# Moving the border inside a tile's mixing in a layer that gathers expert rows

## The reference

```
h = layer_norm(x)
proj = h @ w_in                                # 2824 columns
y_a = window_attention(q, k, v, sinks)         # 8 heads, window of two chunks of 64
y_b = gated_rmsnorm(gated_delta_rule(silu(conv(qkv))), z)   # 4 heads of 128, state over chunks
h = layer_norm(ALPHA * h + concat(y_a, y_b) @ w_out)
scores = (h @ w_query) . sub_keys              # 8 heads x 2 x 128 keys
expert = top 16 of the sums of the top 16 of both halves    # 128 experts for each token
act = gelu(expert_u[expert] . h) * softmax(best)
out = layer_norm(ALPHA * h + sum(act * expert_v[expert]))
```

## Time and profile before

| | |
|---|---|
| time, median of 3 runs | 3772.17 us (3769.79 to 3791.0) |
| the profiled execution: time | 3825.0 us |
| its span, first to last instruction | 3823.2 us |
| mean granted TensorE clock | 0.731 of full speed |
| busy: PE, DVE, POOL, ACT | 2165.8, 2152.2, 2080.4, 380.1 us |
| moved by DMA | 1191.73 MB, mean 312 GB/s |

### The profile page before, as it was taken

One profiled execution on the slowest core, in us unless ns is written; L12 is line 12 of the kernel. 1 busy time (PEld: TensorE's weight loads), 2 busy tenths in 40 slices (PEclk: granted clock), 3 DMA queues, 4 the chain that ended last, 5 costly groups with the idle time before them and its releaser, 6 DMA issues. The chain is left out here.

```text
span 3823.2 us, 34475 instructions
## 1 busy us (share of the span) xinstructions
PE 2165.8 (57%) x9905; PEld 1092.6 (29%) x9905; DVE 2152.2 (56%) x6670; ACT 380.1 (10%) x697; POOL 2080.4 (54%) x2079
## 2 busy tenths in 40 slices
PE   6999967646656566735663554556653333323355
PEld 4665745224243232213321231123211000100111
DVE  4342567766667676566755765577656554444300
ACT  3321132011010010001000100010000000000000
POOL 0000046646536566666665656666656666666664
PEclk9999988767767767767776677667776565555677
DMA  8423168978859799989998999889989999999997
GB/s 281 133 77 109 48 216 298 361 263 334 321 182 362 282 330 388 379 335 338 356 399 325 342 333 403 337 322 355 404 326 362 352 365 360 348 364 369 349 369 291
DMA packets 400102, 1191.73 MB, mean 312 GB/s; under 512 B 54737, under 2 KB 122658, under 8 KB 397986
## 3 DMA queue, kind: packets, MB, share of 16 engines
q0 software_dynamic: 294912, 1073.87, 75.0%
q1 hardware_dynamic: 39970, 75.66, 5.5%
q10 hardware_dynamic: 65024, 39.89, 3.6%
HBM read 1168.27 MB, written 21.00 MB: 311 GB/s over the span
## 5 line engine op out<-in xcount | busy, mean ns | idle before, releaser
L948 POOL DMA_INDIRECT U<-in_expert_u,eidx x1024 | 1046.8, 1022 | 556.5 <-issue 286.0
L1330 PE MATMUL bank<-V,ZH 128*32 128x512 f32 x3712 | 714.0, 887 | 918.2 <-DMA V<-in_expert_v,eidxT 717.5
L2094 DVE CUSTOM_DVE_ANT_0 U<-U,h1c 128x512 f32<-128x512 f32 x1368 | 871.3, 689 | 538.6 <-DMA U<-in_expert_u,eidx 432.2
L956 POOL DMA_INDIRECT V<-in_expert_v,eidxT x832 | 835.3, 1004 | 549.3 <-POOLq L954 302.2
L1330 PEld LDWEIGHTS bank<-V,ZH 128*32 128x32 f32 x3712 | 141.4, 141 | 1394.1 <-issue 1392.0
L2083 DVE CUSTOM_DVE_ANT_0 U<-U,h1c 128x1024 f32<-128x1024 f32 x256 | 303.2, 1224 | 58.9 <-DMA U<-in_expert_u,eidx 42.5
L304 PE MATMUL bank<-V,U 128*128 128x387 f32 (+2 forms) x1056 | 316.1, 459 | 12.4 <-PEq L302 12.2
L978 POOL COPY eidx<-eidx_n 128x128 uint32<-128x128 uint32 x8 | 3.4, 430 | 443.2 <-POOLq L977 443.2
L304 PEld LDWEIGHTS bank<-V,U 128*128 128x128 f32 x1056 | 201.3, 193 | 117.4 <-issue 20.8
L1135 PE MATMUL bank<-wq,arena 128*128 128x512 f32 x400 | 197.1, 642 | 47.7 <-PEq L1258 32.7
L1088 PE MATMUL bank<-arena 128*128 128x512 f32 x224 | 124.8, 704 | 39.0 <-DMA arena<-in_w_out 17.3
(11 more groups left out here) (301 smaller groups left out, 2726.5 us busy)
## 6 DMA issues: line engine op xcount, KB each, us to landing
arena<-in_w_out SPq DMA_DIRECT2D x56, 512.0 KB
U<-in_w_in ACTq DMA_DIRECT2D x36, 512.0 KB, 3.9
U<-in_expert_u,eidx POOLq DMA_INDIRECT x1024
V<-in_expert_v,eidxT POOLq DMA_INDIRECT x928
raw<-proj_dram SPq DMA_DIRECT2D x8, 1344.0 KB
wq<-in_w_query SPq DMA_DIRECT2D x4, 2048.0 KB, 16.1
proj_dram<-U ACTq DMA_DIRECT2D x42, 192.0 KB, 1.9
arena<-w_dram SPq DMA_DIRECT2D x6, 1024.0 KB
```

What stands on the lines that cost most here:

```text
L948: pool.indirect_dma_start(U[:, c % NU, :], None, expert_u[0], rows(ap=eidx[:, e, c:c + 1], axis=0)).then_inc(g_u[c % NU], 16)
L956: pool.indirect_dma_start(V[:, c % NV, :], None, expert_v[0], rows(ap=eidxT[:, e, token:token + 1], axis=0)).then_inc(g_v[c % NV // 2], 16)
L1330: last = nc.tensor.matmul(acc_ps[NSTEP * j:NSTEP * j + NSTEP, 512 * n:512 * n + 512], Zb[:, at - i:at - i + NSTEP], buf[j][:, 512 * n:512 ...
L2094: ins = nc.vector.tensor_tensor_reduce(out=U[:, c % NU, lo:lo + D // 2], in0=U[:, c % NU, lo:lo + D // 2], in1=rows[:, lo:lo + D // 2], sc ...
```

## The change

The point at which a segment takes over a tile's mixing moves from its start to its middle. A loop segment t now does pieces 12 to 36 of tile t + 1 (table `BACK`, halves 9 to 38; PE starts with piece 11 at half 8), then the tail of tile t + 1 (`TAIL`, halves 40 to 57), and beside it pieces 0 to 11 of tile t + 2 (`FRONT`, halves 39 to 61; piece 11 of PE comes in the next segment). Segment 1 does only pieces 0 to 11 of tile 3 (`NEXT_FRONT`, halves 31 to 62), and tile 2's tail is placed somewhat otherwise (`FIRST_TAIL`, 32 to 56). Segment 6 (`ahead` = 1) does pieces 12 to 36 and the tail of tile 7. At the head of a segment PE waits for the new values of the chunk (`b_vnew`) where it had waited for the scores to be read; that wait now stands at PE's half 40. ACT copies the next tile's rows (`rows_ahead`) behind its piece 22 and no more at the head of the segment. SP's list in a turn becomes: first two slices (`first_slices`), the store, the residual rows and the other slices of tile t + 3, and then raw of tile t + 4. DVE no longer waits for the store in piece 1 (`b_pr_free` is gone).

```diff
--- before.py
+++ after.py
@@ -80,18 +80,16 @@
 LATE_MIX = phase(list(range(7, 23)) + list(range(31, 37)),
                  [1, 2, 4, 5, 7, 8, 10, 11, 12, 13, 15, 15, 16, 17, 18, 20, 25, 26, 27, 28, 29, 30])
 LATE_MIX_PE = tensor_phase(LATE_MIX, **route_phase(21, 2), n35=31)
-NEXT_MIX = phase(list(range(23)) + list(range(31, 37)),
-                 [31, 33, 34, 35, 36, 37, 38, 39, 40, 41, 43, 44, 45, 46, 47, 48, 49, 51, 51, 53, 55, 56, 57,
-                  61, 61, 63, 63, 63, 63])
-NEXT_MIX_PE = tensor_phase(NEXT_MIX, **route_phase(59, 2))
-FIRST_TAIL = phase(range(37, 50), [33, 34, 38, 40, 42, 44, 46, 48, 50, 52, 54, 60, 61])
-FIRST_TAIL_PE = {48: 60, 49: 62}
-MIX = phase(list(range(23)) + list(range(31, 37)),
-            [7, 9, 11, 13, 15, 17, 19, 21, 23, 25, 27, 29, 31, 33, 35, 36, 37, 39, 39, 41, 43, 45, 47,
-             53, 55, 57, 59, 61, 63])
-MIX_PE = tensor_phase(MIX, **route_phase(49, 1))
-TAIL = phase(range(37, 50), [1, 3, 10, 14, 18, 20, 22, 26, 28, 30, 32, 50, 52])
-TAIL_PE = {48: 51, 49: 54}
+FIRST_TAIL = phase(range(37, 50), [32, 33, 35, 36, 38, 40, 41, 43, 44, 46, 47, 55, 56])
+FIRST_TAIL_PE = {48: 53, 49: 57}
+NEXT_FRONT = phase(range(12), [31, 34, 37, 39, 42, 45, 48, 51, 54, 57, 60, 62])
+NEXT_FRONT_PE = tensor_phase({n: half for n, half in NEXT_FRONT.items() if n < 11})
+BACK = phase(list(range(12, 23)) + list(range(31, 37)), [9, 11, 13, 14, 15, 17, 17, 19, 21, 23, 25, 31, 32, 35, 36, 37, 38])
+BACK_PE = tensor_phase(BACK, n11=8, n35=40, **route_phase(27, 1))
+TAIL = phase(range(37, 50), [40, 42, 44, 45, 45, 46, 46, 48, 48, 50, 50, 56, 57])
+TAIL_PE = {48: 55, 49: 60}
+FRONT = phase(range(12), [39, 41, 43, 45, 47, 49, 51, 53, 55, 57, 59, 61])
+FRONT_PE = tensor_phase({n: half for n, half in FRONT.items() if n < 11})
 FOLD_SLOT, FOLDS = 1, 2
 SUM_AT, ROWS_AT = 4, 6
 CONVS = range(6, 18)
@@ -749,7 +747,6 @@
         b_wo_free0 = sem("b_wo_free0")
         b_wo_free1 = sem("b_wo_free1")
         b_pre_in = sem("b_pre_in")
-        b_pr_free = sem("b_pr_free")
         b_pr_done = sem("b_pr_done")
         b_tok_raw = sem("b_tok_raw")
         b_squared = sem("b_squared")
@@ -896,11 +893,17 @@
                     sp.dma_start(raw[:, :, :], proj_dram[:, :, bass.ts(t, P)]).then_inc(b_raw, 16)
                     sp.dma_start(akt[:, :], ak_dram[:, bass.ds(t * P, CHUNK + P)]).then_inc(b_raw, 16)
 
-                def more_loads(t):
+                def first_slices():
+                    for k in range(2):
+                        sp.wait_ge(b_wo_free1 if k % 2 else b_wo_free0, 1)
+                        sp.sem_inc(b_wo_free1 if k % 2 else b_wo_free0, -1)
+                        sp.dma_start(wo[k % 2], wo_v[k]).then_inc((b_wo1 if k % 2 else b_wo0), 16)
+
+                def more_loads(t, first=0):
                     sp.wait_ge(b_pr_done, 1)
                     sp.sem_inc(b_pr_done, -1)
                     sp.dma_start(pre[:, :], h_dram[t]).then_inc(b_pre_in, 16)
-                    for k in range(KD - 2):
+                    for k in range(first, KD - 2):
                         if k == 4 and streamed(t):
                             sp.wait_ge(w_stored, 16)
                             sp.wait_ge(w_free, 1)
@@ -928,13 +931,18 @@
                         sp.wait_ge(b_projected, 1)
                         sp.sem_inc(b_projected, -1)
                     loads(t)
-                    more_loads(t)
+                    if t < 3:
+                        more_loads(t)
                 with sp.Fori(0, T - 4) as t:
+                    first_slices()
+                    store(t)
+                    more_loads(t + 3, 2)
                     loads(t + 4)
-                    store(t)
-                    sp.sem_inc(b_pr_free, 1)
-                    more_loads(t + 4)
-                for t in range(T - 4, T - 1):
+                first_slices()
+                store(T - 4)
+                sp.sem_inc(t_free, 1)
+                more_loads(T - 1, 2)
+                for t in range(T - 3, T - 1):
                     store(t)
                     sp.sem_inc(t_free, 1)
                 store(T - 1)
@@ -1365,12 +1373,13 @@
                         for half in (2 * s, 2 * s + 1):
                             if ahead > 0:
                                 at(TAIL_PE, half, t + 1)
+                                at(BACK_PE, half, t + 1)
                             if ahead > 1:
-                                at(MIX_PE, half, t + 2)
+                                at(FRONT_PE, half, t + 2)
                         weighted(t - 1, s)
                         if s == 0:
                             if ahead > 0:
-                                piece(35, t + 1)
+                                pe.wait_ge(b_vnew, 1)
                             norm_rows(2, t_ln)
 
                 pe.wait_ge(b_load, 80)
@@ -1408,7 +1417,7 @@
                     for half in (2 * s, 2 * s + 1):
                         at(LATE_MIX_PE, half, 2)
                         at(FIRST_TAIL_PE, half, 2)
-                        at(NEXT_MIX_PE, half, 3)
+                        at(NEXT_FRONT_PE, half, 3)
                     if s % 2:
                         weighted(0, NSTEP // 2 + s // 2)
                 with pe.Fori(0, T - 4) as t:
@@ -1601,16 +1610,17 @@
                     weights()
                     root()
                     norm()
-                    if ahead > 0:
-                        act.wait_ge(b_hx_free, 1)
-                        act.sem_inc(b_hx_free, -1)
-                        rows_ahead()
                     for s in range(USEG):
                         for half in (2 * s, 2 * s + 1):
                             if ahead > 0:
                                 at(TAIL, half, t + 1)
+                                at(BACK_PE, half, t + 1)
+                                if BACK_PE[22] == half:
+                                    act.wait_ge(b_hx_free, 1)
+                                    act.sem_inc(b_hx_free, -1)
+                                    rows_ahead()
                             if ahead > 1:
-                                at(MIX_PE, half, t + 2)
+                                at(FRONT_PE, half, t + 2)
                         if 4 <= s <= 24 and s % 4 == 0:
                             fill(1 + s // 4)
 
@@ -1829,8 +1839,6 @@
                         dve.wait_ge(s_dve, 1)
                         dve.sem_inc(s_dve, -1)
                         dve.sem_inc(b_root_in, 1)
-                        dve.wait_ge(b_pr_free, 1)
-                        dve.sem_inc(b_pr_free, -1)
                         pad()
                         soften(0, t)
                     elif n == 2:
@@ -2170,12 +2178,12 @@
                         elif half == ROWS_AT + 1:
                             norm()
                         if ahead > 0:
+                            at(BACK, half, t + 1)
                             at(TAIL, half, t + 1)
                         if ahead > 1:
-                            at(MIX, half, t + 2)
+                            at(FRONT, half, t + 2)
 
                 dve.sem_inc(b_raw_free, 1)
-                dve.sem_inc(b_pr_free, 4)
                 dve.sem_inc(b_h1n_free, 1)
                 dve.sem_inc(w_yfree, 1)
                 dve.sem_inc(g_accfree, 1)
@@ -2211,7 +2219,7 @@
                     dot(1, 2 * half + 1)
                     at(LATE_MIX, half, 2)
                     at(FIRST_TAIL, half, 2)
-                    at(NEXT_MIX, half, 3)
+                    at(NEXT_FRONT, half, 3)
                 with dve.Fori(0, T - 4) as t:
                     segment(t + 2, 2)
                 segment(T - 2, 1)
```

## The result

The changed kernel takes 3823.46 us (median of 4 runs, 3806.63 to 3837.43) where the kernel before takes 3781.59 us (3769.79 to 3792.03): ratio 1.0106, 95% interval 1.0063 to 1.015. It is slower, by 1.1%, and the interval excludes a ratio of 1; the forecast was 3705 us and faster, with a range that ended at 3778. The profiled execution of the changed kernel took 3806.6 us, 17 us under its median, and that of before 3825.0, 43 us over its own. So the two traces, laid side by side, show a gain of 18 us that the timed runs don't have, and a segment of the first comparison may carry several us of luck: segment 7, which is the same in both kernels, differs by 6. Later traces were needed for the sizes.

A forecast was written before the change was run, and what follows sets the result against it. The prediction took segment 1 to be bound by DVE's chain and the loop to sit 20 to 30 us above its gathers; -64 + 15 - 20 = -69 on the profiled 3825.0 gave 3756, about 3705 as median, range 3650 to 3778.

The forecast's parts named there:

- What bounds the kernel now: Whole kernel: segment 1 bound by DVE's chain, loop segments some 20 to 30 us above the pace of their gathers.
- Part 1: Segment 1: pieces 12 to 22 and 31 to 36 of tile 3 leave it, -64 us (bounds 50 to 75).
- Part 2: Segment 6: it gets pieces 12 to 36 of tile 7 and 5.6 MB of loads, +15 us (bounds +5 to +30).
- Part 3: Loop segments 2 to 5: new order of pieces gives 395 us each, -5 a segment, -20 for four.
- The 198: Loop segment, halves 31 to 58 (top-k, tail, pieces 0 to 9): 198 us, between 158 of work alone and 219.
- halves 0 to 8 need 29 (the rows fetched ahead cover them): Loop segment, first nine halves: 29 us once pieces 37, 38 and 0, about 14 us, are removed.
- rival (c): Segment 1 gains, but loop segments take 405 to 412 us and give back half to all: 3742 to 3772; chance 0.24.
- Rival (b): Crowded stretch paces everything at 8.2 us a half: loop segment 426 us, +55 in all, 3827; chance 0.10.
- its turning point: Rival of the pacing stretch: the sign turns when a loop segment exceeds 413 us, from 7.7 us a half.
- Rival (a): Crowded stretch hidden under the gathers: loop segments 380 us, -129 in all, 3643; chance 0.08.
- Rival (d): Segment 1 keeps its length, bound by PE or the front pieces' chain: gain 25 instead of 64, 3742; chance 0.06.
- The conversion: Whole kernel: profiled execution 53 us above the runs' median, same difference taken after, so 3756 becomes about 3705.

The follow-up runs named there:

- fast chip: Pace of two groups of follow-up runs, in which the kernel before takes 3513 or 3514 us and a gather 1.29 us.
- b_again: The kernel before, unchanged, timed and traced again in the first follow-up group: 3513.02 us, ratio 1.0006.
- b_more: The kernel before with ten more DVE reductions (13 us in all) in halves 20 to 29 of segments 2 to 7: 3529.75 us, ratio 1.005 to before.
- slow chip: Pace of the other groups of runs, in which the kernel before takes 3782 to 3812 us and a gather 1.42 to 1.46 us.
- two later pairs: Kernel before and changed kernel, both unchanged, traced again: 3513.02 and 3558.15 us in one group, 3823.08 and 3841.55 us (one execution each) in another.
- a_again: The changed kernel, unchanged, timed and traced again in the first follow-up group: 3558.15 us, ratio 1.013 to before.
- the pair at 1.44: Kernel before and changed kernel, both unchanged, traced in the fourth follow-up group, one execution each: 3823.08 and 3841.55 us.

## Why the prediction was wrong

**What bounds the kernel now: read wrongly in part.** "Halves 0 to 38 with DVE as the pacer" rested on a share of 0.84 to 0.93 and the absence of waits for rows. In the trace of the same kernel on the fast chip the waits are nearly as rare in halves 9 to 30 (5.0 us) and the share is 1.02. The forecast sought part of its gain in the 20 to 30 us above the bare gathers; b_again shows 21.5 of them at full DMA, and b_more that two thirds of added work is hidden. For the slow chip of the forecast's own trace this is not tested.

**Part 1: right.** Forecast -64, measured -58 (407.0 to 348.6), and -68 and -70 in the two later pairs. The second half was forecast at 168 us and took 167.4.

**Part 2: right in sign, small.** +15 forecast, +26, +13.5 and +22.9 measured, within +5 to +30. I charged it to bytes; on the fast chip that charge fits (13.9 us for 13.5), on the slow ones it leaves some 8 to 11 us without a cause.

**Part 3: the step that failed.** The sum for a loop segment was 29 + 131 + 198 + 22 + 14 = 394. Measured in segment 3: 48.4 for halves 0 to 8, 130.7 for 9 to 30, 198.0 for 31 to 58, 31.1 for the rest with the border, 408.2 in all. The terms for halves 9 to 30 and for the crowded stretch hold to the microsecond, the last two together are 5 less. The 198 had luck in it: it was picked between 158 and 219, and the other loop segments have 197 to 204. The failed step is "halves 0 to 8 need 29 (the rows fetched ahead cover them)". The 29 are before's 43 us less the 14 of the pieces that left: DVE's work. But nine halves of gathers take 9 x 5.8 = 52 us, and the eight rows of U cover four halves of them, 23 us, only if the ring is full at the border. In before it was filled there, while DVE stood at the border and worked through the top-k (halves 59 to 63 took 54.8 us, five halves of gathers 29), and POOL stopped 9.4 us because no U row was free, so it was full. DVE then ran at 4.8 us a half on rows already there. In the changed kernel the ring fills in the crowded stretch and is drawn down right behind it: halves 51 to 58 took 33.9 us on the fast chip, where gathers need 41. At the border no more rows stand ahead: DVE waited for them, 10.1 us for landings in this trace (15.1 in a_again) and 8 us with no releaser that the profile shows, 5.4 us a half. I took away the stop and kept its yield. So the segment is gathers' pace plus DVE's excess in the crowded stretch, less what the ring gives back behind it (7 of 27 us on the fast chip).

By that account the loss should grow as gathers get faster: it was +25 us a segment at 1.29 us a gather, +16 in the pair at 1.44 and +6 in the first, where single executions differ by several us. The first pair of traces, with loop segments of 406.2 us and 18 us gained in all, is rival (c), at a chance of 0.24: its reason, a bunch of pieces against a ring of four halves, is the one shown here. The timed runs and the later pairs go beyond it. Rival (b) had the mechanism and the sign, at a chance of 0.10 and a pace of 8.2 us a half; 7.1 was enough, because its turning point was worked out with the same wrong 29 us. Rival (a) gave 380. The stretch's busy time is 147 of 198 us in the first trace and 147 of 172.7 on the fast chip, where 28 halves of gathers are 145: the busy time alone would just fit. Over it come, on the fast chip, 8.3 us for landings in halves 31 to 38 and 18 us of handovers and short gaps between instructions. The Trainium skill ("Runtime: NRT & Kernel Launch", "Instruction fetch mechanics") says that fetching straight code is mostly hidden. The fast chip's trace agrees: no idle time of DVE without a releaser in that stretch. In the first trace it is 12.3 of 51 us, and no run shows what it is. The prediction's step from this rule to 380 us was wrong either way, since the rule says nothing of handovers. Rival (d) fell with segment 1. PE's wait at half 40 was not the cause: POOL waited for U rows, hardly for V.

**The conversion** from the profiled execution to the median added a constant 53 us. The two traces differed from their medians in opposite directions, which is worth 60 us, more than the whole effect; that is why the first pair of traces says -18 and the timed runs +42. Of the 118 us between the forecast 3705 and the measured 3823, 50 lie between the traces' 3756 and 3806.6 (43 of them in the four loop segments, 11 in segment 6) and 68 in this conversion; the other segments cancel but for some 3. The sign doesn't hang on it: a_again is 45 us slower in timed runs.

## What to carry to other kernels

When two streams run side by side through a short ring, work out for each stretch of some ring lengths which is slower, and add the slower one's time; an average over the segment, or a sum of one engine's work, gains time that the ring can't hold. A stretch without waits for transfers isn't proof that the engine paces it: look whether the DMA share is full too, and add a known piece of work there to learn what a microsecond costs at that place (here 13 us cost 13.6, 4.4 or 1.0). And a stop whose removal is counted as gain must have its yield, the transfers that ran on meanwhile, taken off elsewhere.

## What the runs showed of the hardware that was not expected

The same 256 gathers of 512 KB (segment 7) take 331 us in two groups of runs and 365 to 373 us in the others, and the whole kernel 3513 against 3782 to 3812 us, 8%. Chip number 9 stands in a fast and in a slow group, so the cause may be something else than the chip, for instance other work beside this core; it was not looked into. DVE's dense stretch differs less: 89.5 and 94.7 us in halves 39 to 50. But in halves 31 to 38, the top-k, it took 49.3 against 62.2 us. In the slow groups DVE also stands idle with nothing to wait for that the profile shows: 121 us in the four loop segments of the changed kernel, against under 5 in a_again. Why is open.
